# A hybrid decoder layer: another order of VectorE's work in the four steps that compute gates

## What is computed

```python
u = rmsnorm(x, pre_mix_gain)
rg_x, rg_gate, q, k, v, o, log_i, log_f = split(u @ w_in)        # 3080 columns
xc = conv4(rg_x);  r, i = sigmoid(xc @ gate_r), sigmoid(xc @ gate_i)
a = exp(-8 * r * softplus(-lam));  h = scan(a, sqrt(1 - a*a) * (i * xc))
y_rg = rmsnorm(h * gelu(rg_gate), rg_out_gain)
q, k = silu(conv4(q)), silu(conv4(k))
# mLSTM of 4 heads in chunks: cumulative log gates, running maxima m, decay matrix p
num = (q k^T * p) v + inter_w * q C_prev;  den likewise
h_ml = num / max(|den|, exp(-m))
y_ml = headwise_rmsnorm(sigmoid(o) * h_ml)
x = x + rmsnorm(concat(y_rg, y_ml) @ w_out)
x = x + rmsnorm(relu(rmsnorm(x) @ w_up)**2 @ w_down)
```

## Time and profile before

| | us |
|---|---|
| median of 3 executions | 2398.65 |
| lowest and highest | 2397.99, 2399.24 |
| profiled execution | 2398.41 |
| its span in the trace | 2396.6 |
| mean granted clock of TensorE | 0.984 of full |

### The profile page before, as it was taken

The page is one execution under the profiler, slowest core; times in us unless marked ns, Lnnn a source line. Parts: engine busy times, 40 slices in busy tenths (PEclk is TensorE's granted clock), DMA queues, the critical chain, the costliest instruction groups (busy, mean ns, idle before and its releaser), DMA issues.

```text
span 2396.6 us, 29507 instructions
## 1 busy us (share of the span) xinstructions
PE 2297.9 (96%) x10549; PEld 1890.8 (79%) x10549; DVE 1285.9 (54%) x1665; ACT 658.3 (27%) x1187; POOL 809.1 (34%) x506
## 2 busy tenths in 40 slices
PE   5999999999995999999999999979899999999998
PEld 4777888888884878888888888867788888888886
DVE  4677657557563555543553453437744534543535
ACT  5665546455553321110110110134201100110112
POOL 6001001001001064643653563421844733743630
PEclk9999999999996999999999999989899999999999
DMA  5346636354524531211111111257311201211203
GB/s 196 115 160 210 214 102 229 108 184 158 176 69 149 176 105 53 71 37 42 61 44 42 54 53 35 88 186 230 119 36 53 63 32 45 70 35 35 70 18 149
DMA packets 119336, 244.03 MB, mean 102 GB/s; under 512 B 8176, under 2 KB 41552, under 8 KB 119280
## 3 DMA queue, kind: packets, MB, share of 16 engines
q1 hardware_dynamic: 90160, 140.15, 17.2%
q0 software_dynamic: 26816, 94.78, 12.6%
q10 hardware_dynamic: 2304, 8.39, 0.9%
HBM read 192.82 MB, written 50.46 MB: 102 GB/s over the span
## 4 chain that ended last, share of the span: by engine, by line
PE 62%; DVE 3%; ACT 1%; issue 1%; DMA 1%; POOL 0%; ACTq 0%; DVEq 0%; SPq 0%; PEldq 0%; POOLq 0%
PE o_ps L1386 21%; PE o_ps L1387 20%; PE o_ps L1388 20%; DVE o_relu L1662 1%; ACT o_ps L1487 1%; DVE o_ff_lo L1666 1%; PE o_ps L1410 0%; DMA o_v_lo<-ylo_d 0%; DVE o_acc L1606 0%; DMA o_w_raw<-in_w_out 0%; DVE o_v_lo L1655 0%; DVE o_h_t L1622 0%; ACT o_ff_hi L1544 0%; DVE o_h_t L1635 0%; DVE o_acc L1600 0%
## 5 line engine op out<-in xcount | busy, mean ns | idle before, releaser
L1355 POOL TENSOR_TENSOR w_hi<-o_w_raw,one 128x1024 fp32r<-128x1024 f32 x100 | 191.6, 1916 | 684.4 <-PE o_ps L1388 587.7
L1386 PE MATMUL o_ps<-o_v_hi,w_hi 128*128 128x512 f32 x1024 | 400.0, 391 | 4.8 <-DVE o_v_lo L1655 4.8
L1387 PE MATMUL o_ps<-o_v_lo,w_hi 128*128 128x512 f32 x1024 | 399.7, 390 | 0.0
L1388 PE MATMUL o_ps<-o_v_hi,w_lo 128*128 128x512 f32 x1024 | 399.6, 390 | 0.0
L1676 DVE TENSOR_TENSOR o_acc<-o_ps,o_acc 128x512 f32<-128x512 f32 x224 | 154.1, 690 | 377.2 <-PE o_ps L1388 376.9
L1662 DVE TENSOR_TENSOR o_relu<-o_relu 128x512 f32<-128x512 f32 x128 | 220.8, 1725 | 181.1 <-ACT o_relu L1541 180.4
L1541 ACT ACTIVATE o_relu<-o_ps 128x512 f32<-128x512 f32 x128 | 76.4, 597 | 872.9 <-PE o_ps L1388 841.5
L445 PE MATMUL m_unit_ps<-u_hi,w_hi 128*128 128x512 f32 x768 | 308.9, 402 | 0.0
L445 PE MATMUL m_unit_ps<-u_hi,w_lo 128*128 128x512 f32 x768 | 300.8, 392 | 0.0
L445 PE MATMUL m_unit_ps<-u_lo,w_hi 128*128 128x512 f32 x768 | 299.5, 390 | 0.0
L1666 DVE TENSOR_TENSOR o_ff_lo<-o_relu,o_ff_hi 128x512 fp32r<-128x512 f32 x128 | 243.4, 1902 | 90.8 <-ACT o_ff_hi L1544 90.8
(11 more groups left out here) (283 smaller groups left out, 3439.6 us busy)
## 6 DMA issues: line engine op xcount, KB each, us to landing
o_w_raw<-in_mlp_w_up POOLq DMA_DIRECT2D x64, 512.0 KB, 4.6
o_w_raw<-in_mlp_w_down POOLq DMA_DIRECT2D x64, 512.0 KB, 3.5
u_hi<-uhi_d SPq DMA_DIRECT2D x12, 2048.0 KB, 10.6
u_lo<-ulo_d SPq DMA_DIRECT2D x12, 2048.0 KB, 15.0
w_raw<-in_w_in POOLq DMA_DIRECT2D x24, 512.0 KB, 5.5
m_rows<-rows_d SPq DMA_DIRECT2D x16, 512.0 KB, 5.0
o_v_hi<-yhi_d SPq DMA_DIRECT2D x16, 512.0 KB, 5.4
o_v_lo<-ylo_d SPq DMA_DIRECT2D x16, 512.0 KB, 6.2
```

What stands on the lines that cost most here:

```text
L1355: pool.tensor_tensor(w_hi[i], w_raw[i % 2][:], one_bc, ALU.mult).then_inc(w_split[i], 1)
L1386: nc.tensor.matmul(dst, sh, mh, start=(i == 0), stop=False)
L1387: nc.tensor.matmul(dst, sh, ml, start=False, stop=False)
L1388: last = nc.tensor.matmul(dst, sl, mh, start=False, stop=(i == n - 1))
```

## The change

VectorE's list gets another order in the steps 0 to 3, and ScalarE's list one moved instruction. No instruction is added, removed or resized.

- The low parts of the first three u tiles, which stood behind `chunk_locals`, stand ahead of it.
- `rg_output` and `head_total`, which stood behind the convolution of x and the maxima, stand ahead of `chunk_locals` too, behind those low parts.
- `head_output` and the next three low parts come right behind `chunk_locals`, then the maxima, and only then the convolution of x with the copy of its history.
- ScalarE takes the root of the heads' total ahead of the copy of unit o, not behind it.

Steps without gates keep their order.

```diff
@@ ScalarE, period
                 if mix:
                     square_rg(m)
                     square_on(m)
+                if mix and gates:
+                    root_2(m)
                 if project:
                     take("o")
                 high_parts_x(4)
-                if mix:
+                if mix and not gates:
                     root_2(m)
                 if project:
                     take("g")
@@ VectorE, period
                 if mix:
                     head_numerator(m)
                 if gates:
+                    low_parts_x(3)
+                    if mix:
+                        rg_output(m, g_m)
+                        head_total(m)
                     chunk_locals(p)
                 low_of("v")
-                low_parts_x(3)
+                if gates:
+                    if mix:
+                        head_output(m)
+                    low_parts_x(4)
+                    chunk_maxima(p)
                 if project:
                     convolve("x", p, g_p)
                     keep_history(p)
-                if gates:
-                    chunk_maxima(p)
-                if mix:
+                if mix and not gates:
                     rg_output(m, g_m)
                     head_total(m)
                     head_output(m)
-                low_parts_x(4)
                 low_of("x")
                 if mix:
                     rg_square_sums(m)
```

## The result

The changed kernel takes 2411.78 us (median of 6, 2410.86 to 2415.30) against 2399.36 us for the kernel before on the same chip: ratio 1.0053, 95% interval 1.0040 to 1.0066. The forecast was 2410.5, 12.1 over the kernel before; measured are 12.4, and the interval reaches from 9.6 to 15.8. The profiled execution of after took 2413.71 us with a span of 2411.9.

What follows compares the result with a forecast made beforehand. TensorE, busy 96% of the span, was taken as the bound. Step 0's 2.63, steps 1 and 2's 2.34, step 3's 2.03 and the clock's 5.13 us add 12.13 to 2398.41: 2410.5 us, range 2404 to 2416.

Steps and rivals of the forecast that it cites:

- The bound: TensorE, busy 96% of the span; delays in steps with gates reach the end, with an unchanged 486.7 us behind them.
- The wait for the locals: TensorE at L555 waits for VectorE's late chunk locals: 2.63, 3.51, 3.51 and 3.90 us in steps 0 to 3.
- VectorE's wait for den2: VectorE idles ahead of the locals until ScalarE's last square: 1 us in step 1, 1.5 in step 3.
- What comes back: Steps 1 and 2: 0.79 us at the transposes of x, 1.55 in the tail; net loss 1.17 us each.
- The clock: TensorE's clock falls behind the new waits of steps 0 to 2, 1.71 us each, 5.13 in all; step 3's already paid.
- rival B: TensorE's clock costs more, 2.46 us at up to four places: 2413.5 us, up to 2416; chance 0.15.
- The sum: Whole kernel: 2.63 + 2.34 + 2.03 + 5.13 = 12.13 us slower, 2410.5 us.

Runs made afterwards that it cites:

- e3: Kernel before with rg_output and head_total alone moved ahead of chunk_locals, and ScalarE's root ahead of the copy of o: 2409.28 us, ratio 1.0036.
- e11: Changed kernel with head_total moved behind chunk_locals and ScalarE's root back behind the copy of o: 2405.21 us, ratio 1.0020 to the kernel before.
- e1: Changed kernel with chunk_locals alone put back right behind the numerator, ahead of low parts, rg_output and head_total: 2396.45 us, ratio 0.9981 to the kernel before.
- e2: Kernel before with only the first three low parts moved ahead of chunk_locals: 2405.98 us, ratio 1.0022.
- e7: Kernel before with six 128x512 matmuls added in step 3's wait for the locals: 2401.23 us, ratio 1.0002.
- e4: Changed kernel with 10, 14, 14 and 16 matmuls added ahead of the wait for the locals in steps 0 to 3: 2405.38 us, ratio 1.0020 to kernel before.
- e10: e5 with low_of("k") back in its old place in step 3: 2393.17 us, ratio 0.9971 to the kernel before.
- e6: Changed kernel with step 0 alone in the old order, locals ahead of the low parts: 2407.66 us, ratio 1.0038 to the kernel before.
- e5: e8 with the chain of locals split, its first three operations run earlier in steps 0 to 2: 2399.13 us, ratio 1.0000 to the kernel before.
- e8: Kernel before reordered: whole locals behind the numerator, then low parts, rg_output, head_total, convolution last; step 3's low part of w_k behind locals: 2400.37 us, ratio 1.0002.
- e9: e10 with six 128x512 matmuls added in step 3's wait for the locals: 2394.86 us, ratio 0.9979 to the kernel before.

## Why the prediction held, point by point

*The bound.* TensorE's order, and that a delay in the steps with gates reaches the end, held: step 4 starts at 245.73, forecast 245.4. Not quite as forecast, TensorE is busy for 486.10 of the 486.74 us that follow: in step 4 it waits 0.24 us (L492) and 0.41 us (L445), which it does not before. In the traces of e3 and e11 the same two waits stand, in those of e1, e2 and e7 neither, so these 0.6 us look like a cost of the change, and the prediction had put that stretch down as unchanged. Why they arise is open.

*The wait for the locals.* The step that carried the sum: 2.55, 3.45, 3.46 and 3.89 us against 2.63, 3.51, 3.51 and 3.90. That den2 and not the u tiles sets the 3.5 us is shown by e3 (3.45 without u tiles) and e11 (2.16 without den2). e1 shows that the whole loss hangs on the place of `chunk_locals`. VectorE's wait for den2, forecast as 1 us in step 1 and 1.5 in step 3, is 0.87 and 1.44.

*What comes back.* 0.79 and 1.55 us in steps 1 and 2: with the clock taken out (e4), 1.21 and 1.22 us of net loss are left where 1.17 was worked out. In e10, which keeps the gain without the price, the steps are 2.27 and 2.28 us shorter, forecast 2.34.

*The clock.* The fall behind each wait came. e4 is 7.6 us less over its kernel before than the changed kernel, and all four falls cost 7.65. That they agree to the tenth is chance, since each median is known to some 2 or 3 us; by the step lengths e4 is 2.69, 1.45 and 1.39 us shorter in steps 1 to 3, where the falls cost 2.89, 1.62 and 1.49. Its size was off in two places: step 1 had the clock low for 6 us and lost 2.89 (rival B's case, taken as 2.46), step 3 only 1.49, because part of its low stretch lay inside the wait (the granted clock over 237.50 to 237.95, still idle, is 0.55). Such a long fall is no property of step 1: in e3 and e6 it came in step 2, 0.56 over 6.13 us and 0.57 over 6.08. New cost 1.65 + 2.89 + 1.62 + 1.49 - 1.72 = 5.93 us instead of 5.13. The Trainium skill (TensorE: Matmul & The Clock Gate, "Why this matters for your kernels") advises against idle gaps of TensorE beyond about 3 us. Shorter gaps were not safe here: the clock fell behind waits of 1.76 us in e2 and of 2.16 us in e11.

*The sum.* 6.9 us of waits net (2.55 in step 0, and from e4's step lengths 1.21, 1.22 and 51.19 - 51.00 + 1.72 = 1.91) and 5.9 of clock are 12.8, medians say 12.4. The mechanism and each wait held; that the total came within 0.3 us is partly luck, since the clock cost 0.8 us more than forecast and the measurement is no finer than its interval. The profiled execution itself is 15.3 us longer in its span; 12.5 of that lie ahead of step 4, the other 2.8 behind it (2166.2 against 2163.3). Of these, 0.6 are the two new waits of step 4. The rest I take for scatter: the profiles of all these kernels lie between 2162.1 and 2166.9 there, with no order by edit that I can see, but one trace of each does not prove it.

*What stays open.* The medians of e5 and e8 are 3 us higher than their step lengths make them, e10's is 2 us lower. For e8 the trace has the excess behind step 4 (2166.9 against 2163.3) and 0.8 us in the opening. e5's profiled execution is its fastest (2395.96, 3.2 under its median), e10's its slowest (2396.79, 3.6 over), so these two traces do not show what their medians hold. A fall in the opening (last section) costs some 2 to 3 us and may be part of it; that is not shown.

## What to carry to other kernels

Ahead of moving work forward in an in-order queue, look up who waits for what it displaces and by how little that is early: here the displaced chain had 0.16 us to spare, and the moved step brought a wait for another engine along, so nothing short of 3.5 us was to be expected. Count a new idle stretch of the matmul engine with the clock, then test that part by filling the stretch with matmuls. A stall that is removed pays only if the next result is early too: the same fill shortened the step by 0.0 us before y_tok was made earlier and by 1.6 us after.

## What the runs showed of the hardware that I had not expected

The length of a wait does not decide by itself whether the granted clock falls behind it. Ahead of the first transposes of x in step 0, TensorE waits for ScalarE's copy of v (L530) behind the matmuls of a unit. That wait ends between 60.6 and 61.6 us in all thirteen traces, and TensorE comes to it sooner or later. The clock fell behind waits of 2.05 us (e11), 2.82 (e1), 3.07 (e10) and 3.45 (e2). It stayed at 1.00 behind waits of up to 1.16 us (before, e7, e8) and behind 1.94 (e3), 2.45 (the changed kernel), 2.60 (e4), 2.65 (e5), 2.73 (e6) and 3.00 (e9). From e10, then e11, then e9:

```profile
61.00:67.00 6.00, 6.00 (x21) 5.25 (x22) 5.72 (x13) 2.39 (x4) 0.00 (x0) 0.51 0.13 51
```

```profile
61.08:66.00 4.92, 4.92 (x21) 4.38 (x22) 3.33 (x6) 2.40 (x4) 0.00 (x0) 0.65 0.04 16
```

```profile
61.00:67.00 6.00, 6.00 (x33) 5.18 (x34) 5.72 (x13) 2.12 (x4) 0.00 (x0) 1.00 0.14 55
```

What decides it there is open; no run varies it. In e10 the fall costs 0.49 x 6.00 = 2.9 us, which the start of step 1 shows: 78.80 against 75.92 in e9, a kernel that up to there differs in nothing that runs. At L555, where square sums or transposes stand around the wait, the traces agree: the clock fell behind each of the 19 unfilled waits of 1.63 us or longer and behind none of those of 0.29, 0.54, 0.55, 0.94 and 1.29 us.
